# Moving the return reads of a mixture of experts ahead of the last expert's down weights, and four of the sums ahead of its gate-up product's turn

## The chip, the cores and the metric

The kernel runs on one core of a Trainium2 chip, in one launch. The metric is the device time of that launch in microseconds. The kernel before was run three times: 2091.01, 2081.25 and 2087.24 us, median 2087.24 us. The execution that was profiled took 2091.2 us; its span in the trace is 2089.4 us.

## The reference, cut to what matters

Two transformer blocks over 512 tokens of width 1024, all in float32. The first block and the first half of the second one (dense feed-forward, sparse and stick-breaking attention, mLSTM and differential attention) are not touched. What the change touches is the end of the second block, a mixture of 32 experts of which each token uses two:

```python
weights = g_w[:, None] * jax.nn.softmax(top_vals, axis=-1)
...
def expert_block(args):
    xb, e = args
    hid = jax.nn.silu(xb @ w_gate[e]) * (xb @ w_up[e])
    return hid @ w_down[e]
...
y = jnp.sum(y_buf[dest].reshape(T, TOP_K, D) * weights[..., None].astype(h.dtype), axis=1)
...
x = x + hierarchical_moe(h, ...)
```

The w_gate and w_up of an expert are 1024 x 512, its w_down is 512 x 1024: 6 MB of float32 an expert, all of it read from HBM once.

## The kernel before

**An expert.** Each of the 32 experts gets one block of up to 64 token rows (`BLK`); further blocks, up to 15, would run in regions that are skipped when no expert has more than 64 rows. The profiled execution has 64 loads each of w_gate, w_up and w_down, two for each of the 32 blocks, so no further block ran. An expert n is four kinds of steps, in `moe()`: `project(n, 0)` and `project(n, 1)`, the gate and up products of the two halves of the contraction, with the weights as the moving operand and the rows as the stationary one; `turn_hid(n)`, in which TensorE transposes the gate-up product (its copy is the tile `guS`), ScalarE takes the silu and VectorE multiplies into the tile `hF`; and `down(n)`, the down product, first from the weights c = 0, then from c = 1. Its result is evicted to the tile `yo` by ScalarE and VectorE.

**How results come back.** For experts 0 to 29 GpSimd scatters the 64 rows of `yo` into the DRAM tensor `pair_results` (1024 rows, two for each token; the semaphores are `yst0` and `yst1`). At the end SyncE reads it back as eight pieces of 512 KB (the "returns"), and VectorE adds each, times its tokens' weight, into `xt` (the `sum` steps, eight instructions of 128x1024). Experts 30 and 31 take no such way: one product of `yo` with a weighted one-hot matrix `oh` (the `spread` step, eight matmuls of 128x512) gives their part for all tokens, and eight additions of 128x512 on VectorE (`add`) put it into `xt`. Each is followed by its output DMA of 256 KB.

**Who sets the order.** Each engine walks the same list of steps and takes what is its own, so the place of a step in the list is its place in the engine's program. SyncE issues all weight loads on one queue, in the order of the list `units`. They go through a ring of 17 slots of 8 KB a partition (the `large` tiles), each a 1 MB transfer; a load waits until the matmuls of the slot's last user are done. The returns use slots of the same ring, two pieces in one slot. In the SyncE program a loop loads `units[4:M3.main]`, all weights of the main experts; then two waits follow for the scatters of experts 28 and 29 (`yst0`, `yst1`), then the eight returns. The ends of the order, per step list before: `turn_hid(31)`, `down(31)`, `sums(0, 8)`, `spread(31)`.

**Lines.** All matmuls are recorded at line 183 and transposes at 186, since small helpers issue them; L189 is ScalarE's activation, L195 VectorE's tensor_tensor (the `hF` product and the final additions), L201 its scalar_tensor_tensor (the sums), L210 its copy, L225 any direct DMA, L228 an indirect one. So the tile names tell the steps apart: `large<-w_down` is a load for a down product, `large<-pair_results` a return, `bank<-large,xF` a gate or up product, `bank<-mats,guS` the turn, `bank<-large,hF` a down product, `bank<-yo,oh` the spread. A float32 matmul is recorded as two, so eight matmuls stand as x16.

Of the kernel before, what the change touches and what calls it, by code (L numbers as in the profile page):

```python
# [21 lines left out]
NB = 32  # L22
# [111 lines left out]
class Counts:  # L134
# [15 lines left out]
    def did(self, stream, *key, by=1):  # L150
        name = stream if by == 16 else self.OWN.get(stream, self.engine)
        n = self.n[name] = self.n.get(name, 0) + by
        if not self.real:
            assert (stream,) + key not in self.at, (stream, key)
            self.at[(stream,) + key] = name, n
        assert self.at[(stream,) + key] == (name, n)
        return self.sem(name), by

    def after(self, stream, *key):
        if not self.real:  # L160
            return None, 1
        name, n = self.at[(stream,) + key]
        return self.sem(name), n
# [73 lines left out]
def build(nc, A, out):  # L237
    with contextlib.ExitStack() as ctx:
# [69 lines left out]
        units = []  # L308
# [947 lines left out]
        def moe():  # L1256
            steps = []
            add = steps.append
            M = Unit()
# [74 lines left out]
            def weights(src, k, n, until):  # L1334

                u = Unit()
                u.i, u.parts, u.size, u.ahead, u.inner, u.whole = len(units), [(0, src)], k * n, ahead[0], False, True
                u.raw = large.take([until])
                u.raw.at = "B%d" % u.raw.at
                u.F = u.raw.t[:, :].rearrange("p (k n) -> p k n", k=k)  # L1340
                units.append(u)
                return u
# [3 lines left out]
            def fetch(n):  # L1346
                xg[n] = M.xg.take(("mm", "xT", n))
                add(Step("fetch", n=n, xg=xg[n]))

            def turn_x(n):  # L1350
                add(Step("turn_x", n=n, xg=xg[n], bank=banks.take(("xT", n))))
# [15 lines left out]
            def source(n):  # L1367
                return functools.partial(of, n) if n < NB else functools.partial(picked, n - NB)
# [3 lines left out]
            def project(n, part):  # L1372

                if part == 0:
                    gu_banks[n] = banks.take(("gucopy", n))
                s = Step("project", n=n, i=part, bank=gu_banks[n])
                s.units = [weights(source(n)(name, part), 4, 512, ("mm", "gu", n, j2, part)) for j2, name in enumerate(("w_gate_2", "w_up_2"))]
                add(s)

            def turn_hid(n):  # L1380
                add(Step("turn_hid", n=n, bank=banks.take(("mhid", n))))

            def down(n):
                s = Step("down", n=n)
                s.bank = banks.take(("yo", n, 1))
                s.units = [weights(source(n)("w_down_2", c), 2, 1024, ("mm", "dn", n, 2 * c + 1, 1)) for c in range(2)]
                add(s)
# [13 lines left out]
            def sums(a, b):  # L1401
                for i in range(a, b, 2):
                    use = large.take([("sum", j % 4, j // 4) for j in (i, i + 1)])
                    for j in (i, i + 1):
                        t = use.t[:, 1024 * (j - i):1024 * (j - i) + 1024]
                        M.yy.append((t, use.before))
                        add(Step("sum", n=j % 4, k=j // 4, t=t))

            M.yy = []
            for n in range(NB):  # L1410
                if n + 1 < NB:
                    project(n + 1, 0)
                turn_hid(n)
                if n + 1 < NB:
                    project(n + 1, 1)
                if n + 2 < NB:
                    turn_x(n + 2)
                if n + NGR < NB:
                    fetch(n + NGR)
                down(n)  # L1420
                if n == NB - 1:
                    sums(0, 8)
                if n == 2:
                    add(Step("count"))
                if n == NB - 2:

                    add(Step("onehot", n=NB - 1))
# [3 lines left out]
            for x in range(NX):  # L1431
                n, first_unit, first_step = NB + x, len(units), len(steps)
# [18 lines left out]
        ffn2 = ffn("w2_gate", "w2_up", "w2_down", "g_ffn2", "norm1")  # L1451
        mix2, M2 = mixer2()
        experts, M3 = moe()
        R = M3.R
        xF, hF, yo, xt, hb, ei = M3.xF, M3.hF, M3.yo, M3.xt, M3.hb, M3.ei
# [1656 lines left out]
        def sp_program(sp):  # L3112
            def load(u, reg=None):
                if u.size > CAP:
                    for e in u.raw.before:
                        sp.wait_ge(*after(*e))
                    src = u.parts[0][1]
                    sp.dma_start(u.F, src(reg) if callable(src) else src).then_inc(*did("land%s" % u.raw.at, u.i, by=16))
                    return
                if u.raw.before:  # L3120
                    sp.wait_ge(*after(*u.raw.before))
                for n, (at, src) in enumerate(u.parts):
                    src = src(reg) if callable(src) else src
                    a, b = src.shape[-2], src.shape[-1]
                    last = n == len(u.parts) - 1
                    sp.dma_start(u.raw.t[0][:, at:at + a * b].rearrange("p (a b) -> p a b", a=a), src).then_inc(
                        *did("land%d" % u.raw.at, u.i, *(() if last else ("part", n)), by=16))

            sp.dma_start(cols[:, :], A["cols"]).then_inc(*did("cols_in", by=16))
            for k in range(4):  # L3130
                sp.dma_start(xT[:, 2 * k:2 * k + 2, :], A["x"][:, 2 * k:2 * k + 2, :]).then_inc(*did("x_in%d" % k, by=16))
                if k == 0:
                    load(units[0])
            nm = len(MATS) * 128
            load(units[1])
            sp.dma_start(mats[:, :, :].rearrange("p a b -> p (a b)"), A["mats"][:, 0:nm]).then_inc(*did("mats_in", by=16))
            load(units[2])
            load(units[3])
            sp.dma_start(rstage[:, :], A["mats"][:, nm:nm + len(RMATS) * 128]).then_inc(*did("rstage", by=16))
            for u in units[4:M3.main]:  # L3140
                load(u)
            for x in range(2):
                sp.wait_ge(*after("yst%d" % x, NB - 4 + x))
            for i, (t, before) in enumerate(M3.yy):
                tt, q = i % 4, i // 4
                at = 512 * q + 128 * tt
                for e in before:
                    sp.wait_ge(*after(*e))
                sp.dma_start(t, y_pairs[at:at + 128, :]).then_inc(*did("back%d%d" % (tt, q), by=16))
            sp.wait_ge(*after("ei",))  # L3150
            count = sp.value_load(ei[0:1, NX:NX + 1], min_val=0, max_val=NX)
            regs = [sp.value_load(ei[0:1, x:x + 1], min_val=0, max_val=NB - 1) for x in range(NX)]

            def region(x):
                seen = dict(sp.passed)
                with sp.when(count, x):
                    for u in units[M3.main:]:
                        if u.x == x:
                            load(u, regs[x])
                    sp.wait_ge(*after("add", NB + x, 7))  # L3160
                    if x == 0:
                        for more in range(1, NX):
                            region(more)
                sp.passed = seen

            region(0)
            for i in range(8):
                c, tt = i // 4, i % 4
                sp.wait_ge(*after("add", NB - 1, i))
                sp.dma_start(out[tt * 128:(tt + 1) * 128, 512 * c:512 * c + 512], xt[:, tt, 512 * c:512 * c + 512]).then_inc(*did("out", i, by=16))  # L3170
            sp.wait_ge(*after("out", 7))
# [6 lines left out]
        for program, done in ((sp_program, "sync_done"), (pe_program, "matmul_done"), (act_program, "scalar_done"),  # L3178
                              (dve_program, "vector_done"), (pool_program, "gpsimd_done")):
            run(program, Lane(None), done)  # L3180
# [79 lines left out]
```

## Time and profile before

| what | value |
|---|---|
| runs of the kernel, median (lowest, highest) | 2087.24 us (2081.25, 2091.01) |
| the profiled execution, its span | 2091.2 us, 2089.4 us |
| TensorE matmuls busy | 1931.8 us (92%) |
| VectorE busy | 932.6 us (45%) |
| ScalarE busy | 706.7 us (34%) |
| mean transfer rate over the span | 168 GB/s |
| transfer rate in eight of the last nine slices (of 52 us each) | 399 to 410 GB/s |

The chain of waits, which goes back from the last instruction, gives TensorE 70% and DMA 18%. The page's slices show two kinds of time: up to about 1560 us TensorE sets the pace and the transfers are light; from about 1620 us on the queue of weight loads is full all the time and TensorE waits a little for each w_up. The change lies in the last 55 us.

### The profile page before, as it was taken

What the parts mean: (1) busy time and instruction counts of PE and PEld (TensorE: products, weight loads), DVE (VectorE), ACT (ScalarE), POOL (GpSimd) and SP (SyncE); (2) the same over time, 40 slices, a digit from 0 to 9 for tenths busy, and PEclk for the clock granted to TensorE, in tenths of its full rate; (3) what the DMA queues carried; (4) which work ended last, traced back from release to release, by engine and by line L of the source; (5) the groups of instructions that cost most, each with busy time, mean ns of one, the idle gap of its engine ahead of it and who ended that gap; (6) DMA issues with size and microseconds to landing.
All of it is one profiled execution on the core that took longest, in us unless ns stands there. A gap on an engine that the chain in (4) does not pass through costs nothing.

```text
span 2089.4 us, 21566 instructions
## 1 busy us (share of the span) xinstructions
PE 1931.8 (92%) x8680; PEld 1376.1 (66%) x8680; DVE 932.6 (45%) x1482; ACT 706.7 (34%) x1153; POOL 85.1 (4%) x115
## 2 busy tenths in 40 slices
PE   8999999989999889999999999999987988888877
PEld 6888887756777767888888887776773333333332
DVE  5443544367557786544344456556770000000003
ACT  5222323344454354332223244455661111111111
POOL 0000000000000001000000000000001111111110
PEclk9999999998989999999999999999998999999998
DMA  6433333252323304333233233122198999999997
GB/s 196 144 95 109 99 93 78 70 76 54 73 56 60 97 21 139 94 93 99 82 111 101 81 105 87 51 56 56 35 343 323 399 401 405 410 408 409 407 409 307
DMA packets 262058, 351.53 MB, mean 168 GB/s; under 512 B 11696, under 2 KB 225712, under 8 KB 237376
## 3 DMA queue, kind: packets, MB, share of 16 engines
q1 hardware_dynamic: 252432, 326.42, 46.7%
q0 software_dynamic: 9520, 23.66, 3.2%
q8 instruction: 71, 1.16, 0.2%
q14 instruction: 35, 0.29, 0.0%
HBM read 337.71 MB, written 20.45 MB: 171 GB/s over the span
## 4 chain that ended last, share of the span: by engine, by line
PE 70%; DMA 18%; DVE 6%; ACT 3%; issue 1%; SPq 1%; POOL 0%; DVEq 0%; POOLq 0%; ACTq 0%
PE bank L183 69%; DMA large<-w_up 15%; PE bank L186 1%; DMA stage<-w_in 1%; SPq L225 1%; DMA token_rows<-hb 1%; DMA large<-pair_results 1%; ACT p L189 1%; DVE PTL L195 1%; DVE y L195 0%; DVE score L201 0%; DMA xg<-token_rows,tok 0%; DVE p L198 0%; ACT wH L189 0%; DVE st L207 0%
## 5 line engine op out<-in xcount | busy, mean ns | idle before, releaser
L183 PE MATMUL bank<-hH,wH 128*128 128x512 f32 x1104 | 445.9, 404 | 16.1 <-DVE stage0L L195 9.7
L183 PE MATMUL bank<-hL,wH 128*128 128x512 f32 x1104 | 439.0, 398 | 0.0
L183 PE MATMUL bank<-large,xF 128*64 128x512 f32 x1024 | 250.1, 633 | 67.3 <-DMA large<-w_up 67.3
L189 ACT ACTIVATE wH<-stage 128x1024 fp32r<-128x1024 f32 (+3 forms) x231 | 227.7, 996 | 106.4 <-PE bank L183 84.3
L183 PEld LDWEIGHTS bank<-hH,wH 128*128 128x128 f32 x1104 | 213.7, 194 | 66.1 <-DVE stage0L L195 9.7
L183 PEld LDWEIGHTS bank<-hL,wH 128*128 128x128 f32 x1104 | 213.3, 193 | 45.9 <-issue 1.9
L183 PEld LDWEIGHTS bank<-large,xF 128*64 128x64 f32 x1024 | 80.4, 145 | 212.1 <-issue 206.1
L210 DVE COPY yo<-bank 64x512 f32<-64x512 f32 x31 | 21.5, 693 | 265.6 <-ACT yo L189 257.9
L183 PE MATMUL bank<-hidH,wH 128*128 128x512 f32 x352 | 137.4, 390 | 2.1 <-DVE stage2L L195 0.9
L183 PE MATMUL bank<-hidL,wH 128*128 128x512 f32 x352 | 137.0, 389 | 0.0
L183 PE MATMUL bank<-large,hF 128*64 128x512 f32 x512 | 119.3, 607 | 2.7 <-DVE hF L195 2.4
L195 DVE TENSOR_TENSOR hF<-sgT,bank 128x256 f32<-128x256 f32 x32 | 13.5, 421 | 195.1 <-ACT sgT L189 195.1
L183 PE MATMUL bank<-hH,stage4L 128*128 128x512 f32 x232 | 91.9, 396 | 0.0
L189 ACT ACTIVATE hidH<-hf 128x512 fp32r<-128x512 f32 x44 | 27.8, 632 | 188.8 <-DVE hf L195 188.8
L183 PE MATMUL bank<-hH,stage2L 128*128 128x512 f32 x224 | 89.2, 398 | 0.0
L183 PE MATMUL bank<-hH,stage1L 128*128 128x512 f32 x224 | 88.4, 395 | 0.0
L183 PE MATMUL bank<-hH,stage0L 128*128 128x512 f32 x208 | 83.3, 401 | 0.0
L183 PE MATMUL bank<-hH,stage3L 128*128 128x512 f32 x208 | 82.0, 394 | 0.0
L201 DVE SCALAR_TENSOR_TENSOR xT<-bank,xT 128x512 f32<-128x512 f32 x32 | 22.1, 692 | 131.5 <-PE bank L183 131.5
L189 ACT ACTIVATE sg<-sg 128x512 f32<-128x512 f32 x60 | 36.9, 628 | 124.9 <-DVE sg L195 124.8
L183 PEld LDWEIGHTS bank<-hidH,wH 128*128 128x128 f32 x352 | 66.1, 188 | 17.4 <-DVE stage2L L195 1.3
L183 PEld LDWEIGHTS bank<-large,hF 128*64 128x64 f32 x512 | 34.0, 138 | 62.6 <-issue 50.5
(488 smaller groups left out, 3256.8 us busy)
## 6 DMA issues: line engine op xcount, KB each, us to landing
large<-w_gate SPq DMA_DIRECT2D x64, 1024.0 KB, 29.3
large<-w_up SPq DMA_DIRECT2D x64, 1024.0 KB, 28.7
large<-w_down SPq DMA_DIRECT2D x64, 1024.0 KB, 29.4
stage<-w_in SPq DMA_DIRECT2D x58, 512.0 KB, 4.7
stage<-w_gate SPq DMA_DIRECT2D x44, 512.0 KB, 3.8
stage<-w_up SPq DMA_DIRECT2D x44, 512.0 KB, 3.8
stage<-w_down SPq DMA_DIRECT2D x16, 512.0 KB, 4.1
pair_results<-zero POOLq DMA_DIRECT2D x8, 512.0 KB, 3.0
```

The lines of the kernel that those rows point to most:

```text
L183: return self.e.matmul(*a, **k) if self.e is not None else Nothing()
L186: return self.e.transpose(*a, **k) if self.e is not None else Nothing()
L189: return self.e.activation(*a, **k) if self.e is not None else Nothing()
L195: return self.e.tensor_tensor(*a, **k) if self.e is not None else Nothing()
L201: return self.e.scalar_tensor_tensor(*a, **k) if self.e is not None else Nothing()
L210: return self.e.tensor_copy(*a, **k) if self.e is not None else Nothing()
L225: return self.e.dma_start(*a, **k) if self.e is not None else Nothing()
```

## The change

In the step list the eight sums move: four to ahead of `turn_hid(31)`, four to behind it, all ahead of `down(31)`. As the ring of slots is dealt out in the order of the list, the returns now get slots 310 to 313 and the weights of `down(31)` slots 314 and 315. In the SyncE program `M.returns` cuts the list of loads: it stops ahead of the two loads of `down(31)`, makes the two waits and the eight returns, and loads the rest after that.

```diff
             for n in range(NB):
                 if n + 1 < NB:
                     project(n + 1, 0)
+                if n == NB - 1:
+                    M.returns = len(units)
+                    sums(0, 4)
                 turn_hid(n)
+                if n == NB - 1:
+                    sums(4, 8)
...
                 down(n)
-                if n == NB - 1:
-                    sums(0, 8)
...
-            for u in units[4:M3.main]:
+            for u in units[4:M3.returns]:
                 load(u)
             for x in range(2):
                 sp.wait_ge(*after("yst%d" % x, NB - 4 + x))
...
                 sp.dma_start(t, y_pairs[at:at + 128, :]).then_inc(*did("back%d%d" % (tt, q), by=16))
+            for u in units[M3.returns:M3.main]:
+                load(u)
```

On SyncE, the transfers from the down weights of expert 30 (slots 308 and 309) to the end of the main loads; `-` is before, `+` the change:

```order
 L225 DMA large_308<-w_down 128x2048
 L225 DMA large_309<-w_down 128x2048
-L225 DMA large_310<-w_down 128x2048
-L225 DMA large_311<-w_down 128x2048
+L225 DMA large_310<-pair_results 128x1024 x2
+L225 DMA large_311<-pair_results 128x1024 x2
 L225 DMA large_312<-pair_results 128x1024 x2
 L225 DMA large_313<-pair_results 128x1024 x2
-L225 DMA large_314<-pair_results 128x1024 x2
-L225 DMA large_315<-pair_results 128x1024 x2
+L225 DMA large_314<-w_down 128x2048
+L225 DMA large_315<-w_down 128x2048
```

The two loads of the last down product stood ahead of the returns, and of the wait for the scatters that stands at the first return; they now stand behind both.

On VectorE, from the one-hot matrices (`oh`) on; `hF_295` is the operand of expert 31's down product:

```order
 L198 TENSOR_SCALAR oh_306<-toks_305,tk_251,ws_252 64x512
 L198 TENSOR_SCALAR oh_306<-toks_305,up_253 64x512
+L201 SCALAR_TENSOR_TENSOR xt_246<-large_310,w_159_254,xt_246 128x1024 x2
+L201 SCALAR_TENSOR_TENSOR xt_246<-large_311,w_159_254,xt_246 128x1024 x2
 L195 TENSOR_TENSOR hF_295<-sgT_293,bank 128x256
 L201 SCALAR_TENSOR_TENSOR xt_246<-large_312,w_159_254,xt_246 128x1024 x2
 L201 SCALAR_TENSOR_TENSOR xt_246<-large_313,w_159_254,xt_246 128x1024 x2
-L201 SCALAR_TENSOR_TENSOR xt_246<-large_314,w_159_254,xt_246 128x1024 x2
-L201 SCALAR_TENSOR_TENSOR xt_246<-large_315,w_159_254,xt_246 128x1024 x2
```

Four sums now stand ahead of the product into `hF_295`, and the sums as a whole read other slots. TensorE's and ScalarE's programs keep their order.

## Rows read from the trace of the kernel before

**Rows 1.** The page's first line.
```profile
span 2089.4 us, 21566 instructions
```

**Rows 2.** Chain of waits, its end: start us, length us, what.
```profile
2064.80 13.96 DMA large<-pair_results
...
2081.79 3.07 DVE xt L195 x5
```

**Rows 3.** Timeline of SyncE's queue: start us, length us, engine, line, transfer, count.
```profile
2032.87 8.96 SPq L225 DMA_DIRECT2D large<-w_down  x4
2060.68 4.56 SPq L225 DMA_DIRECT2D large<-pair_results  x8
```

**Rows 4.** Waits of SyncE's queue, 2030 to 2089 us: total us, times, longest.
```profile
SPq L180 <- DMA pair_results<-yo,pair: 18.8, 1, 18.8
```

**Rows 5.** Tile large, three narrow stretches: ns min/median/max, starts; issue to landing.
```profile
L225 SPq DMA_DIRECT2D large<-w_down x1: 2117/2117/2117, 2035.1 to 2035.1; - x1
...
DMA to landing us min/median/max: 27.9/27.9/27.9
...
L225 SPq DMA_DIRECT2D large<-w_down x2: 2115/2283/2451, 2037.2 to 2039.7; - x2
...
DMA to landing us min/median/max: 28.2/28.2/28.2
...
L225 SPq DMA_DIRECT2D large<-pair_results x1: 434/434/434, 2064.8 to 2064.8; - x1
...
DMA to landing us min/median/max: 14.0/14.0/14.0
```

**Rows 6.** Tiles xt and out, the output DMAs: all eight, then the last.
```profile
DMA to landing us min/median/max: 2.1/2.9/4.1
...
L225 SPq DMA_DIRECT2D out<-xt x1: 467/467/467, 2084.9 to 2084.9; - x1
...
DMA to landing us min/median/max: 4.1/4.1/4.1
```

**Rows 7.** Tile pair_results on GpSimd, 1600 to 2090 us: the scatters of 30 experts.
```profile
L228 POOL DMA_INDIRECT pair_results<-yo,pair x30: 922/923/932, 1607.2 to 2054.3; - x30
...
DMA to landing us min/median/max: 6.3/6.7/7.6
```

**Rows 8.** Stretches: length, busy PE, PEld, DVE, ACT, POOL; granted clock, DMA share, GB/s.
```profile
2059.50:2061.00 1.50, 1.50 (x10) 0.69 (x8) 0.00 (x0) 0.00 (x0) 0.00 (x0) 1.00 0.46 191
...
2068.50:2070.00 1.50, 1.50 (x6) 0.44 (x4) 0.77 (x1) 0.00 (x0) 0.00 (x0) 0.50 1.02 407
...
2076.00:2077.50 1.50, 1.50 (x5) 0.64 (x4) 1.50 (x2) 0.00 (x0) 0.00 (x0) 1.00 0.16 57
```

**Rows 9.** Timeline of TensorE, the end: start, length, tile, count, idle before, releaser.
```profile
2061.25 3.68 PE L183 MATMUL bank<-large,hF 128*64 128x512 f32 x16
2064.86 0.75 PE L186 MATMUL bank<-mats,guS 128*128 128x128 f32 x4
2067.98 5.35 PE L183 MATMUL bank<-large,hF 128*64 128x512 f32 x16 [2.37 <-DVE hF L195]
2074.09 7.11 PE L183 MATMUL bank<-yo,oh 128*128 128x512 f32 x16 [0.76 <-ACT yo L189]
```

**Rows 10.** Timeline of VectorE, the end.
```profile
2067.50 0.42 DVE L195 TENSOR_TENSOR hF<-sgT,bank 128x256 f32<-128x256 f32 x1
2069.23 8.90 DVE L201 SCALAR_TENSOR_TENSOR xt<-large,w,xt 128x1024 f32<-128x1024 f32 x7 [1.30 <-DMA large<-pair_results]
...
2079.99 4.87 DVE L195 TENSOR_TENSOR xt<-bank,xt 128x512 f32<-128x512 f32 x8
```

**Rows 11.** TensorE after its longest idle time: timeline, then a stretch.
```profile
1580.58 1.22 PE L186 MATMUL bank<-mats,xg 64*128 64x64 f32 x8 [11.82 <-DMA xg<-token_rows,tok]
...
1586.00:1587.00 1.00, 1.00 (x4) 0.24 (x2) 0.00 (x0) 0.00 (x0) 0.00 (x0) 0.50 0.00 0
```

## The prediction

> **What bounds the kernel now.** I read the page first, then the end of the chain of waits, SyncE's queue, the landings of single transfers, and the timelines of TensorE and VectorE. The span is 2089.4 us [rows 1]; the change touches only its last 55 us. The chain ends in a return that lands last, and in VectorE's additions [rows 2]: the last of eight returns, the last sum, eight additions, output DMAs. So the returns are late, not the products: TensorE is through with the spread at 2074.09 + 7.11 = 2081.2 us [rows 9] and stands idle for the last 8 us.
>
> Why they are late is the point. SyncE has issued the down weights of experts 30 and 31 by 2041.8 us and then stands in the wait for the scatter until 2060.68 us [rows 3, 4]. Yet that wait costs little, since what it has issued is still under way: the loads land 28 us after their issue [rows 5]. The last load of expert 30 lands at 2035.1 + 27.9 = 2063.0 us, the two of expert 31 at 2037.2 + 28.2 = 2065.4 and 2039.7 + 28.2 = 2067.9 us, the last return at 2064.8 + 14.0 = 2078.8 us. The eight returns (4.2 MB) thus take 10.9 us behind the last load, the two loads (2.1 MB) 2067.9 - 2063.0 = 4.9 us. That is a queue at its own pace with no hole in what lands.
>
> The sixteen transfer engines are not equally far, though. At 2059.5 to 2061.0 us their mean share is 0.46 at 191 GB/s, 1.02 at 407 GB/s once the returns are issued, and 0.16 at 57 GB/s by 2076 us, with the last return still out [rows 8]. So some are through their part of the weights 8 us or more before the last one, and what lands is set by the last one. Its backlog is what counts: it has no hole before 2063.0 us even if the two last loads are not in its queue.
>
> By the Trainium skill, "DMA: Bandwidth & Descriptors", section "Why a DMA increments its semaphore by 16 and not by 1", a transfer runs on up to 16 engines that finish independently, and the waiter passes only when all have. The shares agree. By the mean engine alone the weights would be there before 2060 us and the returns would meet an empty queue; by the rule the slowest engine's order of work is all that matters, and I sum by that.
>
> **The change part by part.**
>
> *The transfers.* Nothing is removed or added: 4.2 MB of returns and 2.1 MB of weights change places behind 2063.0 us. The returns are issued at 2060.68 us as before, since the scatter of expert 29 hangs on its own down product (issue 2054.3, landing 6.3 us later, [rows 7]), and nothing ahead of that has moved. Are they in time for the last engine? An output DMA of 256 KB is issued and landed in 2.1 us [rows 6], so data moves by 2062.8 us, just ahead of 2063.0. Then the returns land until 2063.0 + 10.9 = 2073.9 us, and the two down loads, issued behind the returns at 2065.3 us, at 2076.3 and 2078.8 us (2.5 us apart, as before). The last landing stays at 2078.8 us; only what lands last is another thing. Bounds: the whole 6.3 MB at 407 GB/s is 15.5 us, and from 2062.0 us it would end at 2077.5; a scatter of 7.6 us, the longest of 30 [rows 7], makes it 1.1 us later. Slots cost nothing: 314 and 315 were last used by the down product of expert 28 and the gate product of expert 30, and by 2061.25 us TensorE is already at expert 30's down product [rows 9], which comes behind both.
>
> *What the last landing now has behind it.* Before: one sum, eight additions, the last output, 2078.8 to 2089.4 = 10.6 us. Now the down product of expert 31, the eviction, the spread, an addition and an output. TensorE's gaps: its turn of expert 31 ends at 2065.6 us, and then it has nothing until 2076.3, where it had 2.37 us before. In both cases it comes out at the low clock: after 2.37 us the granted clock was 0.50 at 2068.5 to 2070 us, that is 1.2 GHz [rows 8], and the down product took 5.35 us where the one before, at 2.4 GHz, took 3.68 [rows 9]. I take the same 5.35 us from the landing of the first load, which ends at 2081.65; the second load is in time for that (2078.8 + 1.84, half of 3.68, is 2080.6). Bound above: all of it at 1.2 GHz, 7.36 us, +2.0; after the longest idle time, 11.82 us, the clock was still 0.50 six us after the first instruction, some of it spent in gaps [rows 11].
>
> Then 0.76 us of eviction and 7.11 us of spread [rows 9], which ends at 2089.5 us. The Trainium skill, "TensorE: Matmul & The Clock Gate", Part 1, has the low clock as the default, which activity releases; that speaks against this change, which lays 11 us of idleness ahead of the last products. The sum by that rule is mine; at an unbroken 2.4 GHz it would be 1.7 us less.
>
> *VectorE.* The sums come off the end. The page has the seven in a row at 8.90 / 7 = 1.27 us each, the eight additions at 4.87 / 8 = 0.61 [rows 10]. All eight returns are in at 2073.9 us; the sums start when VectorE is free at 2067.5 us. The fourth return lands about 2063.0 + 10.9 / 2 = 2068.5; four sums end at 2072.6, the product into `hF` (0.42 us, [rows 10]) at 2073.0, and the other four at 2078.1 us. So `hF`, which now stands behind four sums and four transfers, is ready 3.3 us before its weights land at 2076.3: cost nothing, as long as the fourth return lands before about 2074.6. What is queued behind it on VectorE are the other four sums, and only the additions, which wait for the spread anyway, want those. The additions now follow the spread at its pace (7.11 / 8 = 0.89 us each), and the last ends about 0.7 us behind it, at 2090.2 us. The gain: 1.28 + 7 x 0.61 us of VectorE's work leave the path.
>
> *The end.* The last output took 4.1 us from issue to landing when eight were issued one behind another, the median is 2.9 [rows 6]; at 0.89 us apart I take 2.9: 2093.1 us. The span ended 2089.4 - 2084.9 - 4.1 = 0.4 us later: 2093.5 us. Bounds 2.1 and 4.1: -0.8, +1.2.
>
> **The sum.** 2076.3 + 5.35 + 0.76 + 7.11 + 0.7 + 2.9 + 0.4 = 2093.5 us against 2089.4: 4.1 us more. The profiled execution took 2091.2 us, so 2095.3 for such a one; it is the slowest of the runs shown, 4 us above the median. On the median, 2087.24 + 4.1 = 2091.3 us, +0.2%. With all bounds the same way it is +2.0 (-1.3 - 0.8) to +8.4 us (+1.1 + 2.0 + 1.2), or 2089 to 2096 us. The three runs before lie 10 us apart, so their median is itself uncertain by some 4 us. About 0.5%, 10.4 us, is what a measurement can tell from no change.
>
> **The rivals.**
>
> *The low clock lasts through the spread.* Place: down product and spread of expert 31. Price: 2.0 us for the one, 7.1 for the other, 2093.5 + 9.1 = 2102.6 us, +13.2, or 2100.4 on the median: slower by 0.6%. It decides if the clock is not back before about 2083 us. For it: the idle time of 10.7 us, and the 0.50 after 11.82 us [rows 11]. Against it: the spread ran at 1.00 behind 5.35 us of work [rows 8], and here TensorE would work without a gap just as long. The same page of the Trainium skill warns that the clock has been seen stuck at a low level much longer; nothing in these rows shows it.
>
> *The transfers gain.* If the two last loads had taken room from those ahead of them (transfers of one queue side by side instead of in order), taking 2.1 MB out is worth up to 2.1 MB / 407 GB/s = 5.2 us: 2088.3 us, -1.1, or 2086.1. For it: many engines idle at 2060 us [rows 8]. Against: landings come in the order and at the distance of their issue [rows 5], and an idle engine doesn't help the last one.
>
> *The wait for the scatter is on the path now.* Before, 4.9 us of loads lay between 2063.0 us and a hole in the queue; now none. Each us by which SyncE leaves the wait later than 2060.9 costs 1 us in full. With 5 us more than forecast: 2098.5 us, or 2096.3. For it: the wait of 18.8 us is the longest of the queue [rows 4]. Against: 30 scatters took 6.3 to 7.6 us [rows 7]. To be slower by over 0.5% it would need 6.3 us.
>
> *The sums hold `hF` back.* From a fourth return at 2074.6 us on, one for one. With a landing two returns late (2.7 us) still nothing; price 0 to 2 us, so 2095.5 us or 2093.3.
>
> **How the numbers follow.** Forecast, last landing unmoved and the down product behind it: 0.75. Low clock through the spread: 0.05. Transfers gain: 0.10. Scatter on the path: 0.06. Sums hold `hF`: 0.04. The likeliest gives 2091.3 us. The range takes in its bounds, the gain case and the 4 us of the median: 2084 to 2098 us. Slower by over 0.5% are the low clock, and little of the scatter case and of an unlucky median: 0.07. Faster by over 0.5% has no mechanism, since even the gain case gives 1 us: 0.02, for the spread of the runs. Within 0.5%: 0.91.
>
> **What would show it.** Right: the chain ends in a load of w_down, TensorE and the additions, with no return in it; last w_down lands at 2078 to 2080 us, first return near 2064.5; TensorE is idle about 10.7 us ahead of a down product of 5.3 to 7 us; spread of 7.1 us; additions 0.89 us apart. Wrong: w_down landing before 2076 us (the gain) or after 2081 (the hole), a spread of over 9 us, or `hF` later than 2076 us.

## The result and the profile after

The changed kernel took 2097.11 us, median of six runs (2091.17 to 2099.60), beside 2090.09 us for the kernel before (six runs, 2081.25 to 2091.30). The ratio is 1.0037, 95% interval 1.0021 to 1.0052: slower by 0.21 to 0.52%, 4 to 11 us. Two further sets of twelve runs gave 1.0037 (1.0022 to 1.0052) and 1.0027 (1.0011 to 1.0043). The forecast was +4.1 us, or +0.2%, in a range of 2084 to 2098 us, with 2091.3 us as the likeliest. Of the 5.8 us from there to 2097.11 us, 2.9 are the change itself (7.0 us slower instead of 4.1) and 2.9 are that the median of the kernel before rose from 2087.24 us over three runs to 2090.09 over six.

The page's first line, which answers to [rows 1]:

```profile
span 2097.0 us, 21566 instructions
```

The end of the chain of waits, against [rows 2] (start, length, what):

```profile
2066.60 11.63 DMA large<-w_down
2078.23 0.14 issue
2078.37 6.53 PE bank L183 x16
2084.90 0.58 ACT yo L189
2085.48 0.14 issue
2085.61 7.12 PE bank L183 x16
2092.73 0.02 issue
2092.75 0.69 DVE xt L195
```

There is no return in it any more. It is the chain that was forecast: a load of down weights, the down product, the eviction, the spread, one addition. SyncE's queue, against [rows 3] and [rows 4]; the wait for the scatter is 23.0 us instead of 18.8, since SyncE comes to it two loads earlier, and ends at about the same place (2.4 us behind the start of expert 31's second gate-up product, 2.9 before):

```profile
2035.48 4.31 SPq L225 DMA_DIRECT2D large<-w_down  x2
2062.81 3.75 SPq L225 DMA_DIRECT2D large<-pair_results  x8
2066.60 1.18 SPq L225 DMA_DIRECT2D large<-w_down  x2
2087.46 6.34 SPq L225 DMA_DIRECT2D out<-xt  x8
```

The landings of single transfers, against [rows 5]: expert 30's last load, the first return, the two last loads.

```profile
L225 SPq DMA_DIRECT2D large<-w_down x1: 2128/2128/2128, 2037.7 to 2037.7; - x1
DMA to landing us min/median/max: 27.9/27.9/27.9
...
L225 SPq DMA_DIRECT2D large<-pair_results x1: 327/327/327, 2062.8 to 2062.8; - x1
DMA to landing us min/median/max: 4.0/4.0/4.0
...
L225 SPq DMA_DIRECT2D large<-w_down x1: 637/637/637, 2066.6 to 2066.6; - x1
DMA to landing us min/median/max: 11.6/11.6/11.6
...
L225 SPq DMA_DIRECT2D large<-w_down x1: 497/497/497, 2067.3 to 2067.3; - x1
DMA to landing us min/median/max: 13.4/13.4/13.4
```

Expert 30's last load lands at 2065.6 us and the first return 1.3 us behind it, at 2066.85. There is no hole between them, though SyncE stood in its wait. The last loads land at 2078.2 and 2080.7, 12.6 and 15.1 us behind expert 30's last; 13.3 and 15.8 were forecast. The eight returns between them land 1.26 to 1.28 us apart.

TensorE, against [rows 9], with the gate-up product of expert 31 ahead of it:

```profile
2060.41 3.65 PE L183 MATMUL bank<-large,xF 128*64 128x512 f32 x16 [0.63 <-DMA large<-w_up]
...
2067.49 0.75 PE L186 MATMUL bank<-mats,guS 128*128 128x128 f32 x4
2078.37 6.49 PE L183 MATMUL bank<-large,hF 128*64 128x512 f32 x16 [10.13 <-DMA large<-w_down]
2085.61 7.11 PE L183 MATMUL bank<-yo,oh 128*128 128x512 f32 x16 [0.75 <-ACT yo L189]
```

TensorE is idle for 10.13 us, and the down product takes 6.49 us instead of 5.35. The stretches show why, against [rows 8]; the last three numbers are the granted clock, the transfer share and GB/s:

```profile
2061.50:2063.00 1.50, 1.50 (x8) 0.52 (x6) 0.00 (x0) 0.00 (x0) 0.00 (x0) 1.00 0.15 60
2066.00:2067.50 1.50, 1.50 (x9) 0.30 (x5) 0.00 (x0) 0.00 (x0) 0.00 (x0) 1.00 1.01 391
2079.50:2081.00 1.50, 1.50 (x6) 0.33 (x5) 0.74 (x1) 0.00 (x0) 0.00 (x0) 0.50 0.09 38
2082.50:2084.00 1.50, 1.50 (x6) 0.53 (x4) 0.00 (x0) 0.00 (x0) 0.00 (x0) 0.50 0.00 0
```

The clock is at 1.2 GHz (0.50) until 2084.1 us, that is through nearly all of the down product, and back for the spread. The transfer share is down to 0.15 before the returns come, where it was 0.46 in the kernel before [rows 8]. 0.15 of sixteen engines is an estimate of two or three that still had work; the rest had run dry, and as the next landing came without a gap, the last ones had not.

VectorE, against [rows 10]:

```profile
2070.13 4.87 DVE L201 SCALAR_TENSOR_TENSOR xt<-large,w,xt 128x1024 f32<-128x1024 f32 x4
2075.04 0.42 DVE L195 TENSOR_TENSOR hF<-sgT,bank 128x256 f32<-128x256 f32 x1
2075.38 4.87 DVE L201 SCALAR_TENSOR_TENSOR xt<-large,w,xt 128x1024 f32<-128x1024 f32 x4
2086.75 0.69 DVE L195 TENSOR_TENSOR xt<-bank,xt 128x512 f32<-128x512 f32 x1 [6.50 <-PE bank L183]
...
2092.75 0.69 DVE L195 TENSOR_TENSOR xt<-bank,xt 128x512 f32<-128x512 f32 x1 [0.17 <-PE bank L183]
```

`hF` is ready at 2075.5 us, 2.8 us before its weights. The sums are over at 2080.3, and the additions follow the spread.

**How the rest of this text measures.** The profiled executions differ by several us ahead of the change's place, in code that is the same in all kernels. So I count from the start of expert 31's second gate-up product, which is at 2057.80 us before and 2060.41 in the changed kernel; what is left to the end of the span I call the tail. The expectations of a1_sp_only, a2_dve_only, a3_warm and a4_mid count from the landing of expert 30's last load instead, which is 5.1 to 5.2 us later in every profile. Before, the tail is 2089.4 - 2057.8 = 31.6 us, in the changed kernel 36.6. Of the 7.6 us between the two spans, 5.0 are in the tail and 2.6 ahead of it.

### The profile page after: what moved, and what is told of

Read it like the earlier page. It is cut to its first block, busy times and chain, and to the rows that moved or that the text cites. A ratio compares the mean times of both kernels' runs of the same rounds, so it can differ in the third digit from the quotient of the medians.

```text
span 2097.0 us, 21566 instructions
## 1 busy us (share of the span) xinstructions
PE 1934.0 (92%) x8680; PEld 1377.8 (66%) x8680; DVE 932.8 (44%) x1482; ACT 706.6 (34%) x1153; POOL 85.1 (4%) x115
## 4 chain that ended last, share of the span: by engine, by line
PE 70%; DMA 18%; DVE 6%; ACT 3%; issue 1%; SPq 1%; POOL 0%; DVEq 0%; POOLq 0%; ACTq 0%
PE bank L183 69%; DMA large<-w_up 14%; DMA large<-w_down 2%; DMA stage<-w_in 1%; PE bank L186 1%; DMA token_rows<-hb 1%; ACT p L189 1%; SPq L225 1%; DVE PTL L195 1%; DVE y L195 0%; DVE score L201 0%; ACT wH L189 0%; DMA xg<-token_rows,tok 0%; DVE p L198 0%; DVE st L207 0%
```

## The experiments

Each variant was profiled once, the kernel before and the changed one three times. All but the third profile of before come with runs timed beside the kernel before. Ratios are to that, with 95% intervals; the tail is from the profile.

| kernel | ratio | tail us | landing of the last down product's first load, idle time ahead of the product, its length, us |
|---|---|---|---|
| before, three profiles | (1.0007, 0.9993 to 1.0022 against itself) | 31.6, 31.0, 31.2 | 7.6, 2.4, 5.3 |
| changed, three profiles | 1.0037, 1.0037, 1.0027 | 36.6, 37.6, 37.7 | 17.8 to 18.9, 10.1 to 11.2, 6.1 to 6.5 |
| a1_sp_only | 1.0033 (1.0018 to 1.0048) | 36.5 | 18.0, 10.3, 6.4 |
| a2_dve_only | 1.0013 (1.0000 to 1.0026) | 35.0 | 7.6, 9.3, 6.0 |
| a3_warm | 1.0019 (1.0006 to 1.0032) | 37.7 | 19.9, 2.6, 5.35 |
| a6_warm13 | 1.0017 (1.0001 to 1.0034) | 35.6 | 19.1, none (0.4 within it), 4.3 |
| a4_mid | 1.0021 (1.0007 to 1.0036) | 32.9 | 12.7, 7.3, 5.8 |
| a5_mid_hf | 1.0007 (0.9992 to 1.0022) | 31.7 | 12.9, 5.2, 5.5 |
| a7_no_returns | 0.9982 (0.9964 to 1.0001) | 27.7 | 7.6, 2.8, 5.1 |

**The order of the transfers alone.** The eight sums stand behind the `hF` product:

```diff
                     M.returns = len(units)
-                    sums(0, 4)
                 turn_hid(n)
                 if n == NB - 1:
-                    sums(4, 8)
+                    sums(0, 8)
```

> The changed order of the transfers alone; all eight sums stand behind the product into hF and ahead of the down product. I measure the tail, from the landing of expert 30's last down load to the end of the span: 26.4 us before, 31.4 us in the changed kernel. My theory (the cost is in what the last landing has behind it, and the four sums ahead of hF are hidden behind the loads): tail 31.4 us +-0.5, hF product near 2.5 us after expert 30's last load, down product of 5.3 to 6.6 us. Rival (hF held back by four sums is part of the cost): tail shorter than 30.9 us.

The tail is 36.5 us, or 31.3 in the expectation's count, as in the changed kernel, with the `hF` product begun 9.7 us behind the tail's start instead of 14.6. (That is 4.6 us behind expert 30's last load; the 2.5 of the expectation was off, and in the kernel before it is 4.6 too.) TensorE's last products and the `hF` row:

```profile
2075.77 6.42 PE L183 MATMUL bank<-large,hF 128*64 128x512 f32 x16 [10.31 <-DMA large<-w_down]
2082.94 7.11 PE L183 MATMUL bank<-yo,oh 128*128 128x512 f32 x16 [0.75 <-ACT yo L189]
...
2067.35 0.42 DVE L195 TENSOR_TENSOR hF<-sgT,bank 128x256 f32<-128x256 f32 x1
```

So the place of the sums costs nothing beside this order of transfers, and the order of transfers by itself makes the whole loss. The rival would have had a tail 0.5 us or more shorter.

**The order of the sums alone.** SyncE keeps the order of before (its lines are shown against the changed kernel):

```diff
-            for u in units[4:M3.returns]:
+            for u in units[4:M3.main]:
...
-            for u in units[M3.returns:M3.main]:
-                load(u)
```

> The changed order of the sums alone; the transfers keep the order of before (both down loads, then the wait, then the returns). My theory: hF now waits for the fourth return, which lands some 10.3 us after expert 30's last load (2073.3 in the terms of the trace before), so hF is ready 11.7 us after it, the down product runs from there, 5.3 to 6.6 us, then 0.75 + 7.1 + 0.7 + 3.3: tail 29 to 31 us, 3 to 4 us over before. Rival (the sums' place costs nothing, all is in the transfers): tail 26.4 us.

The tail is 35.0 us, 3.7 above the 31.3 of before; in the expectation's count it is 29.8, inside the 29 to 31. The first load is there 9.4 us before `hF` is ready:

```profile
2070.14 5.08 DVE L201 SCALAR_TENSOR_TENSOR xt<-large,w,xt 128x1024 f32<-128x1024 f32 x4 [1.80 <-DMA large<-pair_results]
2075.25 0.42 DVE L195 TENSOR_TENSOR hF<-sgT,bank 128x256 f32<-128x256 f32 x1
...
2075.73 5.99 PE L183 MATMUL bank<-large,hF 128*64 128x512 f32 x16 [9.25 <-DVE hF L195]
```

So the sums ahead of `hF` are a wait that is only hidden because the changed transfers are later still. The rival, that their place never costs, falls. One thing more moves with the sums, the slots: the second of the last loads now waits for a slot that expert 30's gate product frees and is issued 5.8 us behind the first instead of 2.5. It lands 10.2 us behind the tail's start, as before (10.1 to 10.2), so this costs nothing.

**TensorE kept at work.** Extra matmuls ahead of the last down product, 11 and then 13:

```diff
                 s.units = [weights(source(n)("w_down_2", c), 2, 1024, ("mm", "dn", n, 2 * c + 1, 1)) for c in range(2)]
+                if n == NB - 2:
+                    M.down30 = s.units[1]
                 add(s)
...
                     elif s.kind == "down":
+                        if n == NB - 1:
+                            free(s.bank)
+                            for f in range(11):
+                                pe.matmul(s.bank.t[0:BLK, :], hF[(n - 1) % 2][:, 0:BLK], M3.down30.F[:, f % 2, 0:512], start=True, stop=True)
                         pe.wait_ge(*after("mhid", n))
```

> The changed kernel with 11 extra matmuls of 64x512 on weights and hidden rows of expert 30, written to the bank that the last down product overwrites, so that TensorE works through its idle stretch of 10.1 us. Theory (idleness halves the clock for the last down product, 6.5 us instead of 3.7): down product 3.7 to 4.0 us unless its second load binds (it landed 2.5 us after the first, so at least 2.5 + 1.8 = 4.3), tail 31.4 - 2.2 = 29.2 us. Rival (the clock is no cause; the loads set the down product's 6.5 us): tail stays 31.4.

> The changed kernel with 13 extra matmuls in the idle stretch ahead of the last down product instead of 11 (11 took 9.65 us and left 2.6 us of idle time, behind which the down product took 5.35 us). 13 take 11.4 us and end 1.3 us behind the place where the first load landed in the changed kernel (10.2 us from their start). Theory (idleness sets the clock): granted clock 1.00 throughout, down product 3.7 us, tail 36.6 + 1.1 - 2.8 = 34.9 us. If the transfers stall as with 11 (one return 2.6 us late), down product 3.7 to 4.4 us and tail 36 to 37. Rival: down product over 5 us in spite of the work.

With 11 the test missed: the first load landed 2.1 us later than in the changed kernel's first profile, 2.6 us of idle time were left, and the product took 5.35 us, at 0.53 of the clock in its first 3.5 us. The tail is 37.7 us (32.6 in the expectation's count, 29.2 expected):

```profile
2059.20:2069.00 9.80, 9.70 (x23) 2.92 (x22) 9.46 (x11) 0.49 (x2) 0.00 (x0) 1.00 1.02 410
2069.00:2071.50 2.50, 0.00 (x0) 0.01 (x1) 2.31 (x2) 0.00 (x0) 0.00 (x0) 1.00 0.87 367
2071.50:2075.00 3.50, 3.48 (x10) 1.33 (x12) 0.00 (x0) 0.00 (x0) 0.00 (x0) 0.53 0.04 14
```

With 13 the gap is gone, and so is the low clock:

```profile
2068.00:2073.20 5.20, 5.20 (x13) 1.39 (x11) 5.17 (x6) 0.00 (x0) 0.00 (x0) 1.00 1.03 429
2073.20:2077.60 4.40, 3.87 (x16) 1.06 (x16) 0.70 (x1) 0.00 (x0) 0.00 (x0) 1.00 0.16 67
```

The down product then ends 4.4 us behind its first load (2073.1 to 2077.6; it waits 0.43 us for the second one), against 6.6 in the changed kernel's first profile. From the first load to the end of the span it is 35.6 - 19.1 = 16.5 us, against 36.6 - 17.8 = 18.8 (19.1 and 18.8 in the other two): the idleness costs some 2.3 us. The whole tail fell by only 1.0 us from the changed kernel's first profile, since here the first load came 1.3 us later; 35.6 lies between the 34.9 expected and the 36 to 37 for a late return. Whether the extra matmuls themselves delay the landings (19.1 and 19.9 us, 17.8 to 18.9 without them) was not tested. The timed runs are in line with a gain but do not show it: the intervals of the ratios (1.0017 and 1.0019) overlap those of the changed kernel. By the Trainium skill, "TensorE: Matmul & The Clock Gate", Part 1, the low clock is the default and activity releases it. The trace agrees: 0.50 behind 10.13 us of idle time, 1.00 behind matmuls that nobody needs.

**Half of the returns, the loads, the other half.** Four sums ahead of `hF`, four behind the down step:

```diff
                 turn_hid(n)
-                if n == NB - 1:
-                    sums(4, 8)
...
                 down(n)
+                if n == NB - 1:
+                    sums(4, 8)
...
+                if i == 3:
+                    for u in units[M3.returns:M3.main]:
+                        load(u)
```

> Four returns, then the two loads of the last down product, then the other four returns; four sums ahead of hF, four behind the down step. Theory (a queue without holes, so each thing lands at its place in the queue; two ends share the last landing): first down load 7.6 us after expert 30's last load, down product until 13.5, spread until 21.4, last sum at 17, last addition 22, outputs and end 25.3 to 25.8: tail 25.5 us, 0.9 us under before. Rival (transfers behind the wait suffer whatever their order): tail over 28 us.

The expectation counts from expert 30's last load, 5.2 us behind the start of the tail. Things land where the queue has them: the first load at 12.7 - 5.2 = 7.5 us (7.6 forecast), the last return at 15.8. But `hF` was late: its product began 14.6 us behind the tail's start, 1.9 behind its load, and TensorE could go on at 15.1. The tail is 32.9 us, or 27.7 in the expectation's count, between the 25.5 of the theory and the over 28 of the rival; it is the landings that speak for the theory. The next kernel takes the wait for `hF` away, with `hF` ahead of the sums:

```diff
                     M.returns = len(units)
-                    sums(0, 4)
                 turn_hid(n)
+                if n == NB - 1:
+                    sums(0, 4)
```

> Four returns, the two last down loads, four returns, as in a4_mid, but with the product into hF ahead of all sums. In a4_mid hF was ready 14.6 us after the start of expert 31's second gate-up product (all times here are from that), 1.9 us behind its first load (12.7), and the tail was 32.9 us. Theory: hF at 9.5, down product from 12.8 for 5.4 to 5.8 us, spread from 19.2 to 26.3, the last return at 21.0, its sum until 22.3, eight additions until 27.2 (VectorE is the end again, as before): tail 31.4 us, the same as before (31.6 and 31.0). Rival (hF's place costs nothing, the transfers set it): tail 32.9.

The tail is 31.7 us (31.4 expected; 31.0 to 31.6 before) and the ratio 1.0007, with 1 inside its interval: no difference from before that can be told. VectorE, of this kernel:

```profile
2067.07 0.42 DVE L195 TENSOR_TENSOR hF<-sgT,bank 128x256 f32<-128x256 f32 x1
2067.41 4.87 DVE L201 SCALAR_TENSOR_TENSOR xt<-large,w,xt 128x1024 f32<-128x1024 f32 x4
2074.09 1.28 DVE L201 SCALAR_TENSOR_TENSOR xt<-large,w,xt 128x1024 f32<-128x1024 f32 x1 [1.82 <-DMA large<-pair_results]
2076.05 3.83 DVE L201 SCALAR_TENSOR_TENSOR xt<-large,w,xt 128x1024 f32<-128x1024 f32 x3 [0.68 <-DMA large<-pair_results]
2079.80 4.87 DVE L195 TENSOR_TENSOR xt<-bank,xt 128x512 f32<-128x512 f32 x8
```

With a return last and `hF` early, the end is VectorE's again: last sum, eight additions in a row. No order tried beats before; this one ties with it.

**No returns.** The eight returns and their sums are left out, so the output lacks the parts of experts 0 to 29; the wait for the scatter stays ahead of the last two loads:

```diff
-                        dve.wait_ge(*after("back%d%d" % (n, s.k)))
...
-                        dve.scalar_tensor_tensor(xt[:, n, :], s.t, ...)
+                        dve.tensor_scalar(xt[0:32, n, 0:32], xt[0:32, n, 0:32], 1.0, None, ALU.mult)
...
-                sp.dma_start(t, y_pairs[at:at + 128, :])
```

> The changed kernel without the eight returns and without their sums (the parts of experts 0 to 29 are left out of the output; a small VectorE instruction stands for each sum); the wait for the scatter stays ahead of the last two loads. Theory (the wait is hidden; the returns in the queue, 10 us, are what the down product waits for): the two loads land 1.5 to 5 us behind expert 30's last one (5.2 us after the tail's start), so TensorE goes on as soon as hF is there, at 10 us: down product until 15.4, spread 16.1 to 23.2, tail 27.3 us. Rival (the hole behind the wait is what costs): down load not before 13 us, tail over 30 us.

The loads land 7.6 and 10.1 us behind the tail's start, to the tenth where they land before the change (2065.4 and 2067.9, from 2057.8), though they are issued 20 us later, behind the wait. Tail 27.7 us (27.3 expected):

```profile
2053.50 3.65 PE L183 MATMUL bank<-large,xF 128*64 128x512 f32 x16 [0.63 <-DMA large<-w_up]
...
2064.15 5.14 PE L183 MATMUL bank<-large,hF 128*64 128x512 f32 x16 [2.82 <-DVE hF L195]
2070.05 7.10 PE L183 MATMUL bank<-yo,oh 128*128 128x512 f32 x16 [0.77 <-ACT yo L189]
```

So the wait makes no hole that costs when the loads stand right behind it. What holds the down product back in the changed kernel is the returns' 10 us in the queue. It also sizes the returns with their sums: 31.3 - 27.7 = 3.6 us of the time before, and 9.6 us (37.3 - 27.7) of the changed kernel's.

**Controls.**

> The kernel before, unchanged, as a control. The tail is measured from the start of expert 31's second gate-up product on TensorE to the end of the span: 31.6 us before, 36.6 in the changed kernel. Theory (the tail is a fixed chain, and what comes ahead of it drifts by some us from execution to execution): tail 31.6 +-0.7, its start anywhere from 2050 to 2061 us. Rival (the tail itself drifts by several us, so that 5.0 us can be chance): tail off by over 1.5 us.

> The changed kernel, unchanged, as a control beside the kernel before. Theory: tail 36.6 +-0.7 and a median 5 us (0.24%) above that of before. Rival (the change also costs 2 to 3 us ahead of the tail, as the first six runs' 7 us says): median 7 us above, with a tail of 36.6.

> The changed kernel a third time, for its tail and its median. Theory: tail 36.5 to 37.7 us, first down load 17.8 to 18.5, down product 6.3 to 6.5; median 5 to 7 us above before. Rival (the low clock's 6.4 us was chance and 5.35 is usual): down product near 5.35.

> The kernel before a third time, for its tail: 31.0 to 31.6 us if the tail is a fixed chain.

The tails of before are 31.6, 31.0 and 31.2 us, mean 31.3; those of the changed kernel 36.6, 37.6 and 37.7, mean 37.3. The difference, 6.0 us or 0.29%, lies in all three intervals of the ratio; the medians differ by 7.0, 6.4 and 4.7 us. The starts of the tail are 2054.3 to 2057.8 us before and 2048.9 to 2060.4 in the changed kernel, so the 2.6 us ahead of the tail in the first pair are within what executions differ by: c3_after_third starts its tail 9 us before the kernel before's first profile. Some expectations missed by a little. The tail of c2_after_again, 37.6 us, is outside 36.6 +-0.7. In c3_after_third the first load (18.9 us), the down product (6.14) and the difference of the medians (4.7) lie 0.2 to 0.4 us outside theirs. The tail of the changed kernel thus varies by 1.1 us, that of before by 0.6. The down product of the changed kernel in that third profile, then the clock in its first 5 us and in its last one:

```profile
2048.91 3.65 PE L183 MATMUL bank<-large,xF 128*64 128x512 f32 x16 [0.64 <-DMA large<-w_up]
...
2067.91 6.14 PE L183 MATMUL bank<-large,hF 128*64 128x512 f32 x16 [11.18 <-DMA large<-w_down]
...
2067.91:2072.90 4.99, 4.99 (x12) 1.65 (x14) 0.82 (x1) 0.00 (x0) 0.00 (x0) 0.50 0.14 57
2073.00:2074.05 1.05, 1.05 (x6) 0.16 (x2) 0.00 (x0) 0.00 (x0) 0.00 (x0) 1.00 0.00 0
```

## Why the prediction was right, and where a term was off

- *What bounds the kernel.* Right. The last engines' backlog has no hole at the wait, with or without the loads ahead of it: the first return lands 1.3 us behind expert 30's last load in all three profiles, and a7_no_returns has its loads where before had them. The transfers' gain fell: expert 30's last load landed 5.1 to 5.2 us behind the tail's start in both kernels. The late scatter fell too: SyncE left its wait 2.4 to 2.7 us behind the tail's start, 2.7 to 2.9 before.
- *The last landing.* 13.3 us behind expert 30's last load was forecast for the first of the two loads; 12.6, 13.3 and 13.7 us were measured. The last landing is at 20.3 to 21.3 us of the tail, the return's before at 20.2 to 21.0 (a2_dve_only included). It did not move, as forecast. That the 13.3 is met so closely is in part luck. The forecast's 10.9 us for eight returns hold a last return that came 1.95 us behind the one before it; at the 1.27 us of the others it is 10.2. The first profile has just that, and the other two make up the rest by a late return among the first four, which the prediction does not have.
- *The sums ahead of `hF`.* Right that they are hidden (2.8 us to spare in the first profile, 3.3 forecast), shown by a1_sp_only, and that they cost when they are not, shown by a2_dve_only.
- *The down product.* This term was mis-sized: 5.35 us, with the row of before as the model; 6.49, 6.35 and 6.14 us were measured, +1.0 on average. The product before starts at full clock, since the granted clock falls only 0.5 us later, and has it back 3.9 us from its start; the three of the changed kernel start at the low clock and have it back after 5.8, 5.5 and 5.1 us. Each us at 1.2 GHz adds half a us: 1.7 us before, 2.5 to 2.9 in the changed kernel. The longest idle time of [rows 11] had shown a low clock for six us, and I kept it only as a bound. The other direction was off as well: an unbroken 2.4 GHz would not be worth the 1.7 us that the prediction names, since by its own figures the product can't end before 2078.8 + 1.84 = 2080.6 us, 1.0 us earlier. In a6_warm13 that is what held it: 0.43 us of waiting for the second load, and an end 4.4 us behind the first.
- *The low clock through the spread.* Fell: the spread took 7.11 us each time.
- *The outputs.* 3.3 us from the last addition to the end were forecast, 3.6, 4.1 and 4.0 measured, +0.6.
- *The sum.* +4.1 us was forecast for the tail, 6.0 measured: of the 1.9 us between them the two terms above make 1.6, and 0.3 is that the tail of before is 31.3 us on average instead of the 31.6 of its first profile. The median of 2097.11 us is over the 2096 us that the bounds of the sum reach. It lies inside the range, 0.9 us below its top, by the 4 us that the range allows for the median of before, of which 2.9 were used.

## What to carry to other kernels

Here the end of the kernel is one full queue of transfers, and no order of it made the last landing earlier (20.2 to 22.4 us of the tail in all twelve profiles with returns). In such a case count what each candidate has behind the last landing: a return had a sum and eight additions (10.6 us with the outputs), the weight loads a product, an eviction, a spread and an addition (18.8 us from the first of the two, 16.3 from the last landing). Put last what has the shortest chain behind it, and mind that TensorE comes back slower from a wait, as it did here behind 10 us and already behind 2.4. When executions drift by more than the effect, measure from an event just ahead of the change's place.

## What the runs showed of the hardware

- The last down product took 5.1 to 5.35 us behind 2.4 to 2.8 us of idleness, 5.5 and 5.8 behind 5.2 and 7.3 us, 6.0 to 6.5 behind 9 to 11 us; without idleness one takes 3.7. But the length doesn't follow the idle time alone: 6.49, 6.42, 6.35 and 6.14 us stand behind 10.13, 10.31, 10.75 and 11.18 us, so the longest wait had the shortest of the four. In those profiles the granted clock fell 2.2 to 2.6 us behind TensorE's last work and rose 15.9 to 16.2 us behind it, and a product that starts later has less of it at the low clock. What sets the moment of the rise is open.
- Executions of the same code reach the same point 11 us apart (2048.9 to 2060.4 us). Whether that drift differs between kernels was not tried beyond the medians.
- In c2_after_again, c3_after_third, a3_warm and a6_warm13 a return among the first four landed 1.8 to 2.8 us behind the one before it instead of 1.3, and the first of the last two loads came 0.6 to 2.1 us later than in the changed kernel's first profile; in the three profiles of before there was no such gap among the first four, but in two of them the last return came 1.7 and 1.95 us behind the one before it. It may come from engines that had run dry, but that was not tested.
